# Reordering the state-space stage of a two-block transformer kernel: output projection rows between the mixing products, two exponent banks, an earlier rotary step

## The chip, the cores and the metric

The kernel runs on one core of a Trainium2 chip. The metric is the device time in microseconds (us) of one execution; smaller is better. The core has four compute engines with an instruction stream each: TensorE (PE in the profile, its weight loads PEld), VectorE (DVE), ScalarE (ACT) and GpSimd (POOL). A fifth stream, SyncE (SP), only issues transfers here. The engines meet through semaphores. TensorE writes its results into eight accumulation banks of 128 x 512 floats, `bank[0]` to `bank[7]`.

## The reference

512 tokens of width 1024 go through two blocks of two layers each, all in float32. The change touches the first block alone. One of its layers, cut to what matters:

```python
h = rms_norm(x, norm_mix_w[i])
q, k, v, z, xbc_raw, dt_raw = split(h @ w_in[i])          # 512, 128, 128, 512, 1024, 16 columns
q, k = axial_rope(rms_norm(q)), axial_rope(rms_norm(k))   # 8 query heads, 2 key heads of 64
attn_out = softmax(q @ k.T / 8) @ v                       # no mask
xbc = silu(depthwise_conv(xbc_raw, 5 taps) + bias)        # xs 512, B 2*128, C 2*128
dt = softplus(dt_raw + dt_bias)                           # two directions, 8 heads
# state-space scan in 4 chunks of 128 tokens, forward and backward:
#   inside a chunk   y += (C B^T * exp(decays)) @ (xs * dt)
#   between chunks   y += exp(..) * C @ state;   state = decay * state + B^T (xs * dt * ..)
y = (y_fwd + y_bwd + xs * d_skip) * silu(z)
y = y * rsqrt(mean(y * y, per group of 256) + EPS) * ssd_norm_w[i]
x = x + concat(attn_out, y) @ w_out[i]
x = x + (silu(g) * u) @ w_down[i]                         # g, u = rms_norm(x) @ w_gate, w_up; 2816 wide
```

The second block (windowed attention with a sink, differential attention, a convolution in the feed-forward) follows with other weights.

## The kernel before

**Products.** Every large product is three matmuls: activations and weights are split into a high and a low half, and `three` (L1658, L1659, L1660) adds high x high, low x high and high x low into one bank. The weights stream in by groups `g` of 1 MB into two alternating buffers. Of each group ScalarE makes the high half `w_hi` (`split_hi`, L341) and VectorE the low half `w_lo` (`split_lo`, L818), one group ahead of TensorE. TensorE enters a group through `enter(g)`, which waits for its halves.

**Order.** Each engine has one program that is written out by hand, with waits on semaphores between them. So an instruction runs when those in front of it on its engine are through and its semaphore has come, and moving a call in the source moves it in the stream. There is no scheduler.

**The first block's layer**, by groups from `g0`: queries (two groups), keys, values and step sizes, then the *channel stage*: groups `g0+4` to `g0+7` give the 1024 convolution channels as eight tiles `m` of 128 channels, and `g0+8`, `g0+9` the gate `z`. A half group fills one of banks 0 to 3. VectorE frees the bank of tile `m` in `conv_start(m)` (L1068), and adds the five taps with `conv_taps(m)` (L1077, one at each call's start on ScalarE, `conv_middle`, L560). ScalarE applies silu, and TensorE turns the tile to rows (`turn_channels(m)`). Among these calls VectorE also has the step sizes (`finish_dt`, L1089 to L1108: the softplus, with a logarithm that ScalarE computes at L586), the rotary steps `rope_a(t)` (L907 to L927, a 128-row tile `t` of queries and keys each), the low halves, and `state_coefs` (L1124). The last rows of queries that `rope_a(3)` makes are turned and rounded (L935) and then the first attention scores start (L1780).

**Attention** runs 20 half-steps `i`; TensorE is the busy engine there.

**The mixing stage** has eight passes `w = 2c + v`: chunk `c`, head group `v`. TensorE writes the exponents of unit `u` (16 units, two per pass, one per direction) into a bank of `E_BANKS` (L2029, L2030); ScalarE's `decay(u)` turns them to `a_e` (L642) and sets `dec_ready`; VectorE's `mixer(w)` adds the two directions (L1208) and multiplies by the scores `a_sm` (L1214), giving the mixing matrix `a_mx`; TensorE's `y_products(w)` (L2081, 4 matmuls of 64 columns) multiplies it into the bank `Y_BANKS[c % 2]`, on top of the skip term (L2073, from `skip_operand`, L1200). Beside this TensorE makes the chunks' states (`states(j, d)`, L2049), `scores(c)` (L2039) and the carried term `carried(c)` (L2064), which VectorE scales and adds (L1225 to L1232), then takes the products out (`take_y`, L1239) and gates them (`gate_y`, L1247). ScalarE squares the gated rows (`group_squares`, L662), VectorE makes the variance (`y_var`, L1253), GpSimd the factor (`group_factors`, L1548) and ScalarE applies it (`y_norm`, L670), which sets `yn_done`.

**Output projection.** `w_out` goes through four groups `g0+10` to `g0+13` (`IN_A = 10`). A half group is 8 row tiles `k`: 4 of the attention output `a_ot_hi`, `a_ot_lo`, ready early, and 4 of the normalised state-space output. `part(g, half, ks)` issues three matmuls per `k`. It runs the attention rows of the first two groups (2 groups x 2 halves x 4 x 3 = 48 matmuls), then waits for `yn_done`, turns the gated output on TensorE (L1763), and does the rest. The feed-forward follows.

## Time and profile before

| | us |
|---|---|
| runs | 2453.41, 2454.48, 2456.26 |
| median | 2454.48 |
| profiled execution | 2454.91 |
| its span in the trace | 2452.8 |

| engine | busy us | share |
|---|---|---|
| TensorE | 2397.9 | 98% |
| TensorE weight loads | 1977.3 | 81% |
| VectorE | 1437.0 | 59% |
| ScalarE | 933.7 | 38% |
| GpSimd | 249.6 | 10% |

The mean granted TensorE clock is 0.995 of full speed, and the transfers move 84 GB/s on average. How to read it: TensorE is busy nearly all the time, so its few pauses decide, not the other engines' shares. A row of a timeline gives the start of a group of like instructions in us, its length, engine, line, operation, operands (out<-in, partitions x elements) and their count; in square brackets stands the idle time in front of it and what ended that, by engine, tile and line. Matmuls are pipelined, so a row's length includes time in which the next is already under way. A releaser with a q (DVEq) is that engine's sequencer. The first block's second layer does the same work as its first, about 612 us later.

### The profile page before, as it was taken

The numbers are of one execution on the slowest core, as the hardware profiler recorded it, in microseconds if no ns is written. First come the engines' busy times: TensorE is split into PE (matmuls) and PEld (weight loads), VectorE is DVE, ScalarE is ACT, GpSimd is POOL, SyncE is SP. The second block draws the span as 40 slices with busy tenths as digits, with TensorE's granted clock in tenths as the row PEclk, the third lists the DMA queues.
The fourth block names the chain that finished last, engine by engine and source line by source line (L and its number), as shares of the span: only waits on it lengthen the run. The fifth ranks groups of instructions, "written<-read, shape, count | busy, mean of one in ns | idle before, by whom it ended". The sixth has DMA issues, their size and how long they took to land.

```text
span 2452.8 us, 30923 instructions
## 1 busy us (share of the span) xinstructions
PE 2397.9 (98%) x12492; PEld 1977.3 (81%) x12492; DVE 1437.0 (59%) x1976; ACT 933.7 (38%) x1468; POOL 249.6 (10%) x183
## 2 busy tenths in 40 slices
PE   8999999999999899999999999999999999999999
PEld 7777888888887688888887778888888777888887
DVE  6876543435587644343567766555466776655554
ACT  5564322223456432222344653222244475322222
POOL 3001100000200110000142411000012212000000
PEclk9999999999999999999999999999999999999999
DMA  5210222223211022222321102222232111222222
GB/s 186 69 36 18 103 86 103 88 101 105 102 69 36 18 103 96 93 103 87 111 95 69 36 28 93 103 88 101 99 107 89 67 36 43 95 101 89 103 89 101
DMA packets 31101, 205.32 MB, mean 84 GB/s; under 512 B 3440, under 2 KB 3568, under 8 KB 7408
## 3 DMA queue, kind: packets, MB, share of 16 engines
q1 hardware_dynamic: 30960, 203.35, 23.6%
q8 instruction: 99, 1.62, 0.3%
q14 instruction: 42, 0.34, 0.0%
HBM read 201.24 MB, written 2.10 MB: 83 GB/s over the span
## 4 chain that ended last, share of the span: by engine, by line
PE 87%; DVE 9%; DVEq 1%; issue 1%; ACT 1%; ACTq 0%; POOL 0%; DMA 0%; SPq 0%
PE bank L1658 26%; PE bank L1659 26%; PE bank L1660 26%; PE bank L1780 2%; PE bank L1841 2%; PE bank L1817 2%; DVE a_conv L1077 1%; DVE neg_max L1460 1%; PE bank L1763 1%; PE bank L1828 1%; DVE b_p L1472 1%; PE bank L2226 1%; DVE w_lo L818 1%; DVE h_mix_lo L935 1%; PE bank L2250 0%
## 5 line engine op out<-in xcount | busy, mean ns | idle before, releaser
L818 DVE TENSOR_TENSOR w_lo<-w_raw,w_hi 128x2048 fp32r<-128x2048 f32 (+1 forms) x180 | 411.1, 2284 | 392.8 <-ACT w_hi L341 392.1
L1658 PE MATMUL bank<-h_ffn_hi,w_hi 128*128 128x512 f32 x1408 | 549.2, 390 | 0.0
L1660 PE MATMUL bank<-h_ffn_hi,w_lo 128*128 128x512 f32 x1408 | 548.5, 390 | 0.0
L1659 PE MATMUL bank<-h_ffn_lo,w_hi 128*128 128x512 f32 x1408 | 548.4, 389 | 0.0
L341 ACT ACTIVATE w_hi<-w_raw 128x2048 fp32r<-128x2048 f32 (+1 forms) x180 | 340.9, 1894 | 451.9 <-PE bank L1660 424.0
L1660 PEld LDWEIGHTS bank<-h_ffn_hi,w_lo 128*128 128x128 f32 x1408 | 264.4, 188 | 55.1
L1658 PEld LDWEIGHTS bank<-h_ffn_hi,w_hi 128*128 128x128 f32 x1408 | 264.4, 188 | 54.5
L1659 PEld LDWEIGHTS bank<-h_ffn_lo,w_hi 128*128 128x128 f32 x1408 | 264.5, 188 | 54.3
L1659 PE MATMUL bank<-act_lo,w_hi 128*128 128x512 f32 x704 | 274.2, 389 | 0.0
L1658 PE MATMUL bank<-act_hi,w_hi 128*128 128x512 f32 x704 | 274.2, 389 | 0.0
L1660 PE MATMUL bank<-act_hi,w_lo 128*128 128x512 f32 x704 | 274.2, 389 | 0.0
L1535 POOL TENSOR_TENSOR sq_sum<-sq_sum,sq 128x512 f32<-128x512 f32 x56 | 95.3, 1701 | 1182.8 <-ACT sq L379 1181.5
L1658 PE MATMUL bank<-w_hi,h_mix_hi 128*128 128x512 f32 (+2 forms) x512 | 189.6, 370 | 9.1 <-DVE h_mix_lo L824 7.7
L482 ACT ACTIVATE act_hi<-up 128x512 fp32r<-128x512 f32 x88 | 55.7, 633 | 370.7 <-DVE up L997 370.7
L1660 PE MATMUL bank<-w_hi,h_mix_lo 128*128 128x512 f32 (+2 forms) x512 | 187.1, 365 | 0.0
L1659 PE MATMUL bank<-w_lo,h_mix_hi 128*128 128x512 f32 (+2 forms) x512 | 187.0, 365 | 0.0
L994 DVE TENSOR_TENSOR up<-bank,rstd_bc 128x512 f32<-128x512 f32 x88 | 60.8, 691 | 193.7 <-PE bank L1660 193.7
L1660 PEld LDWEIGHTS bank<-act_hi,w_lo 128*128 128x128 f32 x704 | 132.2, 188 | 27.5
L1659 PEld LDWEIGHTS bank<-act_lo,w_hi 128*128 128x128 f32 x704 | 132.2, 188 | 27.3
L1658 PEld LDWEIGHTS bank<-act_hi,w_hi 128*128 128x128 f32 x704 | 132.2, 188 | 27.3
L976 DVE TENSOR_TENSOR gate<-bank,rstd_bc 128x512 f32<-128x512 f32 x88 | 60.7, 690 | 118.1 <-PE bank L1660 116.3
L1658 PEld LDWEIGHTS bank<-w_hi,h_mix_hi 128*128 128x128 f32 x512 | 97.0, 189 | 25.1 <-DVE w_lo L1028 7.7
(330 smaller groups left out, 3406.1 us busy)
## 6 DMA issues: line engine op xcount, KB each, us to landing
w_raw<-weights SPq DMA_DIRECT2D x184, 1024.0 KB, 4.8
w_raw<-weights SPq DMA_DIRECT2D x4, 544.0 KB, 3.7
w_raw<-weights SPq DMA_DIRECT2D x8, 256.0 KB, 5.7
residual<-x_in SPq DMA_DIRECT2D x8, 256.0 KB, 5.6
x_out<-residual SPq DMA_DIRECT2D x8, 256.0 KB, 2.0
cst<-consts SPq DMA_DIRECT2D x1, 966.0 KB, 9.1
par_b<-params_b SPq DMA_DIRECT2D x1, 627.0 KB, 10.1
par_a<-params_a SPq DMA_DIRECT2D x1, 244.0 KB, 2.8
```

Source lines behind the costliest of these rows:

```text
L341: nc.scalar.activation(w_hi[s][:, cols], w_raw[s][:, cols], ACT.Copy).then_inc(w_hi_done, 1)
L482: act.activation(act_hi[:, 2 * i + j, :], up[j][:, :], ACT.Identity).then_inc(act_hi_done, 1)
L818: nc.vector.tensor_tensor(w_lo[s][:, cols], w_raw[s][:, cols], w_hi[s][:, cols].bitcast(F32), ALU.subtract).then_inc(w_ready, 1)
L976: nc.vector.tensor_tensor(gate[j][:, 1:SEQ + 1], bank[src][:, :], rstd_bc[:, :], ALU.mult).then_inc(bank_free[src], 1)
L994: nc.vector.tensor_tensor(up[j][:, :], bank[src][:, :], rstd_bc[:, :], ALU.mult).then_inc(bank_free[src], 1)
L1535: nc.gpsimd.tensor_tensor(sq_sum[:, :], sq_sum[:, :], sq[k % 2][:, :], ALU.add).then_inc(sum_done, 1)
L1658: mm(out, ahi, bhi, start=start, stop=False)
L1659: mm(out, ahi, blo, start=False, stop=False)
L1660: return mm(out, alo, bhi, start=False, stop=stop)
L1780: last = mm(bank[S_BANKS[i % 2][par_]][:, 0:nb * P], q_[rows, qs], k_[rows, ks], start=(n == 0), stop=(n == 2 and not masked))
L1817: last = nc.tensor.transpose(bank[PT_BANKS[par_]][:, b * P:(b + 1) * P], probs[u % 2][par_][:, b * P:(b + 1) * P], ident)
L1841: last = mm(bank[4][par_ * HD:(par_ + 1) * HD, j * P:(j + 1) * P], v_of(j // 2, k0 + b), pts[u % 2][par_][:, b * P:(b + 1) * P], start=(b ...
```

## The change

All calls keep their arithmetic but for `finish_dt`, which computes log(1 + p) with a shorter correction (five vector instructions and a wait in place of ten). The rest is order:

- ScalarE splits the high half of `g0+6` ahead of the logarithm, not behind the first channel tile; VectorE splits its low half right behind `finish_dt`.
- `state_coefs` moves from the channel stage to attention half-step 9; the skip operands of chunks 0 and 1 move from the mixing passes to half-step 18.
- `rope_a(3)` moves ahead of `conv_taps(4)`, from behind the low half of `g0+9`.
- TensorE turns channel tile 0 behind the first half of the third channel group, not behind the second.
- The exponents use two banks in place of three (`E_BANKS`) and are issued two per pass at its head; `Y_BANKS` becomes banks 7 and 4.
- 24 of the 48 matmuls of the output projection's attention rows (`out_rows`: first group, both halves) stand between the mixing products: three each in passes 2 to 5, six each in passes 6 and 7. `w_out` then starts with its second group.
- `y_var` of chunks 0 and 1 stands right behind `mixer(4)` and `mixer(6)`; ScalarE's squares of these chunks stand one decay later.

```diff
--- before.py
+++ after.py
@@ ScalarE
                 act.wait_ge(dt_v, 3 * lay + 1)
                 nc.scalar.activation(A["a_dt"][:, 1, :], A["a_dt"][:, 1, :], ACT.Exp, scale=-1.0)
                 nc.scalar.activation(tiny[:, 0:16], par[:, A_ALOG:A_ALOG + 16], ACT.Exp).then_inc(dt_s, 1)
+                split_hi(g0 + 6)
                 act.wait_ge(dt_v, 3 * lay + 2)
                 nc.scalar.activation(A["a_dt"][:, 3, :], A["a_dt"][:, 2, :], ACT.Ln).then_inc(dt_s, 1)
...
                 conv_middle(0)
-                split_hi(g0 + 6)
                 step_logs()
...
-                    nc.scalar.activation(A[f"a_e{w % 2}{d}"][:, :], bank[E_BANKS[u % 3]][:, :], ACT.Exp).then_inc(dec_ready, 1)
+                    nc.scalar.activation(A[f"a_e{w % 2}{d}"][:, :], bank[E_BANKS[u % 2]][:, :], ACT.Exp).then_inc(dec_ready, 1)
...
-                    if u in (8, 12):
+                    if u in (9, 13):
                         group_squares(u // 4 - 2)
@@ VectorE
                 def finish_dt():

-                    nc.vector.tensor_scalar(dt[4], dt[2], -1.0, None, ALU.add)
+                    nc.vector.scalar_tensor_tensor(dt[4], dt[2], -1.0, dt[1], ALU.add, ALU.subtract)
                     dve.drain()
-                    nc.vector.tensor_scalar(dt[5], dt[4], 0.0, None, ALU.is_equal)
-                    dve.drain()
-                    nc.vector.tensor_tensor(dt[4], dt[4], dt[5], ALU.add)
-                    dve.drain()
-                    nc.vector.reciprocal(dt[6], dt[4])
                     dve.wait_ge(dt_s, 2 * lay + 2)
-                    nc.vector.tensor_tensor(dt[3], dt[3], dt[5], ALU.add)
-                    dve.drain()
-                    nc.vector.tensor_tensor(dt[3], dt[3], dt[6], ALU.mult)
-                    dve.drain()
-                    nc.vector.tensor_tensor(dt[3], dt[3], dt[1], ALU.mult)
+                    nc.vector.tensor_tensor(dt[3], dt[3], dt[4], ALU.subtract)
                     dve.drain()
...
                 finish_dt()
+                split_lo(g0 + 6)
                 rope_a(2)
                 conv_start(1)
-                split_lo(g0 + 6)
                 conv_taps(0)
                 conv_start(2)
                 conv_taps(1)
                 remainder_rows()
-                state_coefs()
                 split_lo(g0 + 7)
...
                 conv_start(5)
+                rope_a(3)
                 conv_taps(4)
                 conv_start(6)
                 conv_taps(5)
                 conv_start(7)
                 split_lo(g0 + 9)
-                rope_a(3)
                 conv_taps(6)
                 conv_taps(7)
...
+                    if i == 9:
+                        state_coefs()
+                    if i == 18:
+                        skip_operand(0)
+                        skip_operand(1)
...
-                skip_operand(0)
                 for w in range(8):
                     c, v = divmod(w, 2)
                     mixer(w)
+                    if w in (4, 6):
+                        y_var(c - 2)
                     if w == 0:
...
-                        skip_operand(1)
...
-                    if w in (4, 6):
-                        y_var(c - 2)
@@ TensorE
-                for g in (g0, g0 + 1):
+                for g in (g0 + 1,) if rows_begun else (g0, g0 + 1):
                     enter(g)
...
-                        if g == 2 and half == 1:
-                            turn_channels(0)
-                            turn_channels(1)
+                        if g == 2:
+                            turn_channels(half)
...
-                    j = E_BANKS[u % 3]
-                    if u >= 3:
-                        pe.wait_ge(dec_ready, 16 * lay + u - 2)
+                    j = E_BANKS[u % 2]
+                    if u >= 2:
+                        pe.wait_ge(dec_ready, 16 * lay + u - 1)
...
+                def out_rows(half, k):
+
+                    ws = slice(k * COLS + half * P, k * COLS + half * P + P)
+                    three(bank[half][:, :], w_hi[0][:, ws], w_lo[0][:, ws], A["a_ot_hi"][:, k, :], A["a_ot_lo"][:, k, :], k == 0, False)
+
...
-                exponents(2)
                 pe.wait_ge(r_taken, 4 * lay + 4)
...
                     if w < 7:
+                        exponents(2 * w + 2)
                         exponents(2 * w + 3)
-                    if w < 6:
-                        exponents(2 * w + 4)
...
+                    if w == 2:
+                        enter(g0 + IN_A)
+                        pe.wait_ge(o_ready, 4 * lay + 4)
+                    if 2 <= w < 6:
+                        out_rows(0, w - 2)
+                    if w >= 6:
+                        pe.wait_ge(sm_ready, 4 * lay + 4)
+                        out_rows(1, 2 * w - 12)
+                        out_rows(1, 2 * w - 11)
                     y_products(w)
...
-E_BANKS = (5, 6, 7)
+E_BANKS = (5, 6)
 ST_BANKS = (3, 2)
-Y_BANKS = (0, 4)
+Y_BANKS = (7, 4)
```

TensorE, mixing stage of a layer, from the products of pass 6 to the end of mixing, before (`a_mx` mixing matrices, `a_state` the states for the carried term, `a_ot_hi` attention output, the first rows of `w_out`):

```order
L2081 MATMUL bank<-a_x,a_mx 128x64 x4
L2064 MATMUL bank<-a_state,a_bct 128x256 x2
L2081 MATMUL bank<-a_x,a_mx 128x64 x4
L1658 MATMUL bank<-a_ot_hi,w_hi 128x512
L1659 MATMUL bank<-a_ot_lo,w_hi 128x512
L1660 MATMUL bank<-a_ot_hi,w_lo 128x512
```

The same place now (old L2081 is L2073, L2064 is L2056, L1658 to L1660 are L1651 to L1653):

```order
L2073 MATMUL bank<-a_x,a_mx 128x64 x4
L2056 MATMUL bank<-a_state,a_bct 128x256 x2
L1651 MATMUL bank<-a_ot_hi,w_hi 128x512
L1652 MATMUL bank<-a_ot_lo,w_hi 128x512
L1653 MATMUL bank<-a_ot_hi,w_lo 128x512
L1651 MATMUL bank<-a_ot_hi,w_hi 128x512
L1652 MATMUL bank<-a_ot_lo,w_hi 128x512
L1653 MATMUL bank<-a_ot_hi,w_lo 128x512
L2073 MATMUL bank<-a_x,a_mx 128x64 x4
```

Before, only the carried matmuls stood between the products of passes 6 and 7, and the projection began behind them; now six matmuls of the projection's first rows stand ahead of the last products (and six ahead of those of pass 6).

VectorE, channel stage, before, from the bank read of tile 5 (`a_pad`) on:

```order
L1068 TENSOR_TENSOR a_pad1<-bank,rstd_bc 128x512
L1077 SCALAR_TENSOR_TENSOR a_conv0<-a_pad0,par_a,a_conv0 128x512 x4
L1068 TENSOR_TENSOR a_pad0<-bank,rstd_bc 128x512
L1077 SCALAR_TENSOR_TENSOR a_conv1<-a_pad1,par_a,a_conv1 128x512 x4
L1068 TENSOR_TENSOR a_pad1<-bank,rstd_bc 128x512
L818 TENSOR_TENSOR w_lo1<-w_raw1,w_hi1 128x2048
L907 TENSOR_TENSOR a_m1<-a_q,a_table 128x512
L907 TENSOR_TENSOR a_m1<-a_k,a_table 128x128
L916 TENSOR_TENSOR a_sqs<-a_q,a_table 128x8x16 x4
L916 TENSOR_TENSOR a_sqs<-a_k,a_table 128x2x16 x4
L920 TENSOR_TENSOR a_m1<-a_m1,a_sqs 128x640
L927 TENSOR_TENSOR a_q<-a_m1,head_rs 128x512
```

The same place now:

```order
L1068 TENSOR_TENSOR a_pad1<-bank,rstd_bc 128x512
L907 TENSOR_TENSOR a_m1<-a_q,a_table 128x512
L907 TENSOR_TENSOR a_m1<-a_k,a_table 128x128
L916 TENSOR_TENSOR a_sqs<-a_q,a_table 128x8x16 x4
L916 TENSOR_TENSOR a_sqs<-a_k,a_table 128x2x16 x4
L920 TENSOR_TENSOR a_m1<-a_m1,a_sqs 128x640
L927 TENSOR_TENSOR a_q<-a_m1,head_rs 128x512
L927 TENSOR_TENSOR a_kdup<-a_m1,head_rs 128x128
L927 TENSOR_TENSOR a_kdup<-a_m1,head_rs 128x64
L1077 SCALAR_TENSOR_TENSOR a_conv0<-a_pad0,par_a,a_conv0 128x512 x4
L1068 TENSOR_TENSOR a_pad0<-bank,rstd_bc 128x512
L1077 SCALAR_TENSOR_TENSOR a_conv1<-a_pad1,par_a,a_conv1 128x512 x4
```

The rotary step (`a_m1`, `a_q`, `a_kdup`) stood behind the bank reads of tiles 6 and 7 and the low half; now it is ahead of all three.

VectorE, mixing passes 4 and 5, before:

```order
L1208 TENSOR_TENSOR a_e00<-a_e00,a_e01 128x512
L1214 TENSOR_TENSOR a_mx0<-a_e00,a_sm 128x512
L1225 TENSOR_TENSOR a_y1<-bank,a_pfx 128x512
L1227 TENSOR_TENSOR sq1<-bank,a_pfx 128x512
L1232 TENSOR_TENSOR a_y1<-a_y1,sq1 128x512
L1239 TENSOR_TENSOR a_y1<-a_y1,bank 128x512
L1253 TENSOR_SCALAR tiny<-tiny 128x2
L1208 TENSOR_TENSOR a_e10<-a_e10,a_e11 128x512
```

The same now (old L1253 is L1243):

```order
L1198 TENSOR_TENSOR a_e00<-a_e00,a_e01 128x512
L1204 TENSOR_TENSOR a_mx0<-a_e00,a_sm 128x512
L1243 TENSOR_SCALAR tiny<-tiny 128x2
L1215 TENSOR_TENSOR a_y1<-bank,a_pfx 128x512
L1217 TENSOR_TENSOR sq1<-bank,a_pfx 128x512
L1222 TENSOR_TENSOR a_y1<-a_y1,sq1 128x512
L1229 TENSOR_TENSOR a_y1<-a_y1,bank 128x512
L1198 TENSOR_TENSOR a_e10<-a_e10,a_e11 128x512
```

The variance of chunk 0 moves from behind the carried and summed output (`a_y1`) to right behind the mixing matrix.

ScalarE, mixing stage, as a difference (`a_e` decays, `a_sm` scores, `sq` squares, `a_silu_z` the normalised output):

```order
 L642 ACTIVATE a_e<-bank 128x512 x3
 L650 ACTIVATE a_sm<-bank 128x256
+L642 ACTIVATE a_e<-bank 128x512
 L662 ACTIVATE sq,tiny<-a_y 128x256 x2
-L642 ACTIVATE a_e<-bank 128x512 x3
+L642 ACTIVATE a_e<-bank 128x512 x2
 L670 ACTIVATE a_silu_z<-a_y,tiny 128x256 x2
```

The squares of chunk 0 now come one decay later, and one decay fewer stands between them and the normalisation.

## Rows read from the trace of the kernel before

**Rows 1.** The page's first part: each engine's busy time, share of the span, instructions.

```profile
PE 2397.9 (98%) x12492; PEld 1977.3 (81%) x12492; DVE 1437.0 (59%) x1976; ACT 933.7 (38%) x1468; POOL 249.6 (10%) x183
```

**Rows 2.** TensorE's waits, 789 to 827 us: line <- releaser: us, times, longest.

```profile
PE bank L2081 <- DVE a_mx L1214: 4.9, 5, 2.1
...
PE bank L2064 <- DVEq L1194: 0.9, 1, 0.9
...
PE bank L2029 <- ACT a_e L642: 0.3, 1, 0.3
```

**Rows 3.** Timeline of TensorE, layer 1: start, us, line, operands, [idle before <-releaser].

```profile
821.23 1.11 PE L2081 MATMUL bank<-a_x,a_mx 128*128 128x64 f32 x8 [1.89 <-DVE a_mx L1214]
...
825.66 1.11 PE L2081 MATMUL bank<-a_x,a_mx 128*128 128x64 f32 x8 [2.10 <-DVE a_mx L1214]
...
826.58 0.48 PE L1658 MATMUL bank<-a_ot_hi,w_hi 128*128 128x512 f32 x1
...
836.50 1.03 PE L1763 MATMUL bank<-cst,a_silu_z 128*128 128x128 f32 x8
```

**Rows 4.** Stretches: us, busy PE, PEld, DVE, ACT, POOL, clock, DMA share, GB/s.

```profile
817.00:827.20 10.20, 5.80 (x32) 4.10 (x32) 7.21 (x12) 5.02 (x16) 1.07 (x1) 1.00 0.01 2
...
209.40:219.70 10.30, 9.14 (x28) 7.22 (x27) 6.25 (x12) 4.54 (x14) 2.46 (x3) 0.50 0.00 0
...
827.20:830.70 3.50, 3.50 (x10) 2.75 (x9) 1.62 (x4) 1.90 (x7) 0.86 (x2) 0.51 0.01 5
```

**Rows 5.** Timeline of TensorE, layer 0, end of mixing and first turn.

```profile
213.19 1.97 PE L2081 MATMUL bank<-a_x,a_mx 128*128 128x64 f32 x8 [1.16 <-DVE a_mx L1214]
...
225.44 1.04 PE L1763 MATMUL bank<-cst,a_silu_z 128*128 128x128 f32 x8
```

**Rows 6.** Timeline of ScalarE, layer 1, mixing stage.

```profile
816.14 0.91 ACT L670 ACTIVATE a_silu_z<-a_y,tiny 128x256 f32<-128x256 f32 x2 [4.77 <-POOL tiny L1548]
...
831.27 0.91 ACT L670 ACTIVATE a_silu_z<-a_y,tiny 128x256 f32<-128x256 f32 x2 [1.03 <-POOL tiny L1548]
```

**Rows 7.** Timeline of TensorE, layer 0, channel stage.

```profile
57.14 0.39 PE L1660 MATMUL bank<-h_mix_hi,w_lo 128*128 128x512 f32 x1
...
57.37 0.39 PE L1658 MATMUL bank<-h_mix_hi,w_hi 128*128 128x512 f32 x1
...
71.39 0.50 PE L1658 MATMUL bank<-h_mix_hi,w_hi 128*128 128x512 f32 x1 [0.52 <-DVE w_lo L818]
...
103.74 0.39 PE L1658 MATMUL bank<-w_hi,h_mix_hi 128*128 128x512 f32 x1
...
118.82 0.50 PE L1780 MATMUL bank<-h_mix_hi 64*128 64x512 f32 x2 [1.76 <-DVE h_mix_lo L935]
```

**Rows 8.** Timeline of VectorE, layer 0, channel stage.

```profile
60.11 0.20 DVE L1091 TENSOR_SCALAR a_dt<-a_dt 128x64 f32<-128x64 f32 x1
...
62.80 0.82 DVE L893 TENSOR_REDUCE ssq<-a_squares 128x10 f32<-128x640 f32 x1
...
79.65 0.29 DVE L1124 TENSOR_TENSOR a_coef<-a_dt,a_pfx 128x32 f32<-128x32 f32 x2
...
83.95 0.75 DVE L1077 SCALAR_TENSOR_TENSOR a_conv<-a_pad,par_a,a_conv 128x512 f32<-128x512 f32 x1 [0.86 <-ACT a_conv L560]
...
102.77 0.69 DVE L1068 TENSOR_TENSOR a_pad<-bank,rstd_bc 128x512 f32<-128x512 f32 x1
...
105.99 0.69 DVE L907 TENSOR_TENSOR a_m<-a_q,a_table 128x512 f32<-128x512 f32 x1
...
110.02 1.57 DVE L1077 SCALAR_TENSOR_TENSOR a_conv<-a_pad,par_a,a_conv 128x512 f32<-128x512 f32 x2
```

**Rows 9.** Timeline of ScalarE: layer 0's channel stage, then layer 1's mixing stage.

```profile
60.77 1.90 ACT L341 ACTIVATE w_hi<-w_raw 128x2048 fp32r<-128x2048 f32 x1
...
800.51 1.28 ACT L677 ACT_TABLE_LOAD   x1
...
801.80 1.06 ACT L677 ACTIVATE a_silu_z<-a_silu_z 128x1024 f32<-128x1024 f32 x1
```

More of the change, by code:

```diff
@@ L1846, in pair_attention, with w_out @@
                         behind[i]()
-            def w_out(lay, g0, base, n, ot_hi, ot_lo, src, mixed, count, high_banks):
+            def w_out(lay, g0, base, n, ot_hi, ot_lo, src, mixed, count, high_banks, rows_begun):
                 def part(g, half, ks):
@@ L2120, in _ @@
                         pe.wait_ge(o_free, 4 * lay + 4)
+                    if w == 2:
[7 more added lines that the diff above has]
+                        out_rows(1, 2 * w - 11)
                     y_products(w)
                 pe.wait_ge(dec_ready, 16 * lay + 16)
[L2123 removed]
+                w_out(lay, g0 + IN_A, base, 6, A["a_ot_hi"], A["a_ot_lo"], A["a_silu_z"], yn_done, 4 * lay + 4, (yi_free, 4 * lay + 4), True)
                 feed_forward(lay)
@@ L2252, in _ @@
                         last.then_inc(do_done, 1)
-                w_out(lay, g0 + IN_B, base, 14, B["b_ot_hi"], B["b_ot_lo"], B["b_dm"], mix_ready, l + 1, (do_free, 4 * l + 3))
+                w_out(lay, g0 + IN_B, base, 14, B["b_ot_hi"], B["b_ot_lo"], B["b_dm"], mix_ready, l + 1, (do_free, 4 * l + 3), False)
                 feed_forward(lay)
```

1 line of the change is left out of this document (removed).

## Prediction, written before the changed kernel was run

> **What bounds the kernel now.** First the table of engines: TensorE is busy 98% of the span [rows 1], and the chain of waits that ended last runs through it almost everywhere. So only two things can pay: stretches in which TensorE stands still, and stretches in which it runs at half clock. I went through its timeline for every row with an idle time in front, in the two layers of the first block, the only ones that the change touches. They sit in two places, the same in both layers.
>
> The larger is the mixing stage. Between 789 and 827 us the view of waits puts nearly all of TensorE's idle time down to VectorE's mixing tiles, five waits of 4.9 us together; with one wait of 0.9 and two of 0.3 us the stage has 8 gaps of 6.4 us [rows 2]. The timeline shows the longest: 2.10 us before the last mixing products, at 825.66 [rows 3]. A 512-column matmul's row is 0.39 us long while the next starts 0.23 us after it [rows 7], so each gap costs about 0.16 more than its idle row: 8 gaps, 7.7 us per layer.
>
> Then the clock. In layer 0 TensorE's granted clock is 0.50 (1.2 GHz) for 10.3 us, in layer 1 0.51 for 3.5 us [rows 4], and each stretch begins right behind the long waits at the end of mixing. What it costs is read from one piece of work in both layers, from the start of the last mixing products to the turn of the gated output: 225.44 - 213.19 = 12.25 us in layer 0 [rows 5], 836.50 - 825.66 = 10.84 us in layer 1 [rows 3]. The piece is 0.92 us of mixing products and 36 matmuls at 0.227, 8.16, and 0.1 for the switch: 9.2 at full clock. So the clock costs 3.1 and 1.7 us, together 4.7.
>
> The second place is the channel stage. TensorE waits 0.52 us for a low weight half at 71.39 and 1.76 us for VectorE's last turned query row before the first scores at 118.82 [rows 7]. VectorE is nearly without a pause there.
>
> **The change, part by part.** All times are of one layer; the sum doubles them.
>
> *Channel stage.* The shorter step-size arithmetic first. It now takes 2.69 us, 60.11 to 62.80 [rows 8]. Five of ten instructions stay, at the steps of those rows about 0.3 each for the first three and 0.1 for the last two. But the high half of group g0+6 now stands on ScalarE ahead of the logarithm that they need. It may start when TensorE ends group g0+4, whose last matmul is the one at 57.14 [rows 7], at about 57.6; it lasts 1.90 as at 60.77, a table load behind it 1.28 [rows 9] and a 64-element step some 0.2: 61.0. VectorE, ready at 60.4, waits 0.6 and ends at 61.9, 0.9 earlier than now. Next, the low half of g0+6 follows at once and ends near 64.1, long before TensorE asks for it at 70.9: its wait of 0.52 goes. The state coefficients leave the stage: from 79.65 to 80.02 with the drain in front, 0.45 [rows 8]; in the attention VectorE has room for them. VectorE's wait of 0.86 at 83.95 is for ScalarE behind the channel transposes; the first of these now follows half a group earlier on TensorE, so I let it vanish.
>
> Then the last rotary step, 105.99 to 110.02, 4.03 us [rows 8], is put in front of the fifth channel tile's taps. Queued behind it are taps 4 and 5, the reads of banks 2 and 3 by tiles 6 and 7, and the low half of g0+9. Bank 3 is the tight one. TensorE starts writing it at 103.74 [rows 7], and VectorE gives it free at 102.77 + 0.69 = 103.46 [rows 8]: 0.28 us of slack. With the change VectorE frees it at 103.46 + 4.03 - 0.9 - 0.45 - 0.86 = 105.3, TensorE is there at 103.2, and a new wait of about 2 us opens; I take 1.9. What it buys: VectorE comes to the turned rows 2.2 us earlier, TensorE to the first scores 1.4 later, so the wait of 1.76 closes. Net: -0.5 + 1.9 - 1.8 = -0.4. The ends: without the new wait -2.2; with it and the old wait still open +1.4. A table load rule of the Trainium skill bears on this place. The trace shows a load of 1.28 us at 800.51 and its function's start at 801.80, 1.29 later [rows 9]: the load is the whole price. The Trainium skill (ScalarE: Activation LUTs, section What ACT_TABLE_LOAD costs) adds a drain of about 1.38 us to each switch; by it the logarithm and everything behind it on VectorE would come 1.4 later, and the time is that of the rival below.
>
> *Mixing stage.* Per pass w of eight TensorE issues two exponents, then scores, carried terms and the like, then the mixing products. Three edits take work out of its waits. (a) The skip operands (0.6 us each) go from VectorE's mixing passes into its wait for the last attention block. (b) The group variance of chunks 0 and 1 is taken right behind mixer 4 and 6, no longer behind some 2.9 us of carried and summed output. Now ScalarE waits 4.77 us at 816.14 for GpSimd's factor [rows 6], the decays behind it come late, and TensorE stands 1.89 us before the products at 821.23 [rows 3]; the factor now comes earlier and the squares stand behind one more decay. (c) 24 matmuls of the output projection's first rows, 5.44 us, stand ahead of the products: three each in passes 2 to 5, six each in 6 and 7. In these passes TensorE had five gaps and, from here on, enough work of its own to cover them.
>
> What remains. Passes 0 to 2 get no filler, so the waits for the second and third states and for the first carried term stay, 0.3 to 0.9 in the trace. And one grows: the third exponents now come behind the first states and the skip term, ScalarE's decay 2 stands ahead of its copy of the first states, so the second states wait for the copy, about 1.0. I count 2.8 us of waits left ahead of the last products. They then end 2.8 + 5.44 - 7.7 = 0.5 us later than now.
>
> Behind them the cover is gone. Now 36 matmuls (8.3 us with the switch) hide the chain take, gate, squares, variance, factor, norm: from the end of the products at 826.58 [rows 3] to 831.27 + 0.91 = 832.2 [rows 6], 5.6 us, of which 0.45 is VectorE still busy with chunk 2's variance; I take 5.3. With 12 matmuls left (2.8 us) TensorE waits a new 2.5 us there, and the turn comes 5.3 instead of 8.3 behind the products. Net: +0.5 + 5.3 - 8.3 = -2.5. The ends: -5.0 if the left-over 2.8 us of waits were mostly gone, +2.4 if the fillers hid nothing.
>
> *Clock.* The long waits ahead of the last products go, but a wait of 2.5 takes their place. In layer 1 half clock followed the 2.10 us before 825.66; the 1.89 before 821.23 had left it at full [rows 3, 4], and so had the 1.76 at 118.82 in layer 0 [rows 7]. So I expect a fall again, with dense matmuls right behind it, which is layer 1's case now: 1.7 us, not layer 0's 3.1. Gain 4.7 - 3.3 = 1.4 over both.
>
> *Two exponent banks.* Exponents u waits for decay u-2 instead of u-3, but each pair is issued one slot later, so it waits for the same decays as now; the bank is worth nothing by itself and gives bank 7 to the products so that bank 0 is free for the projection. Later groups of the projection, the feed-forward and the second block keep their work; no DMA is added, and the weights' transfers are not near the path (DMA share 0.01 at the end of mixing [rows 4]).
>
> **Sum.** 2 x (-0.4 - 2.5) - 1.4 = -7.2. Against the profiled execution's 2454.9 us (span 2452.8) that is 2447.7; the median of the runs, 2454.48, lies 0.4 under it, so I give **2447.3**.
>
> **Rivals.** *The clock holds.* If one wait of 2.5 between dense stretches doesn't bring it down, 3.3 more comes back: 2444.0. For it: the 1.76 one was harmless; against: 2.5 is longer than the 2.10 that brought it down. *The fillers only partly hide.* If VectorE's mixing chain, not TensorE, sets the pace to the end, the products come 2.5 later than I say: 2447.3 + 5 = 2452.3. For it: VectorE is busy 7.21 of 10.2 us there [rows 4]. *The channel stage turns bad*: bank 3's wait comes and the first scores still wait: +1.8 per layer, 2451. For it: the slack of 0.28. *Slower: a serial round.* With two banks the exponents of pass w+1 are issued only at the head of pass w. If VectorE is through its other work before these exponents (0.46) and the second decay (0.5) are done, every pass gets longer by 0.96, seven times, 6.7 per layer: 2447.3 + 13.4 = 2460.7. It decides from the point where VectorE's carried work, 3.7 us per pass at most, is shorter than exponents, two decays and two handovers, some 1.8; the rows speak against it in all but the even passes. *The table load* with a drain: +1.4 per layer through bank 3, 2450.1. *The change doesn't do what it says*: the built order shows all the moves; if the gains are given back whole, 2454.5.
>
> **How the numbers follow.** Forecast 0.45, clock holds 0.22, partly hidden 0.13, channel stage 0.08, serial round 0.06, table load 0.03, nothing 0.03. The range takes in the forecast with its terms' play, the clock case and the channel case: 2443.5 to 2451.3, with the serial round, the empty case and most of the partly hidden one left out. A measurement here tells 0.2%, 4.9 us: faster means under 2449.6. Forecast and clock case give 0.67, and of the three cases between 2450 and 2452.3 about 0.09 falls under the line: faster 0.76, within 0.17, slower 0.07.
>
> **What would show it.** In the profile after: no wait for a low weight half before group g0+6; a TensorE wait of 1.6 to 2.1 us on VectorE's channel tile halfway through group g0+8 and none before the first scores; about 1 us before the second states; no wait before the mixing products from pass 2 on; 2.3 to 2.8 us before the first turn of the gated output, with a clock of 0.5 for some 3.5 us behind it; ScalarE's waits for GpSimd's factor near 4.8 gone for chunks 0 and 1. Wrong would be mixing waits left in passes 4 to 7 (then the fillers don't cover) or a first turn without a wait (then the chain is shorter than its rows).

## The result: 14.4 us less, twice the forecast

| | before | after |
|---|---|---|
| median of the runs, us | 2455.22 | 2440.79 (2439.73 to 2443.41) |
| profiled execution, us | 2454.91 | 2443.41 |
| its span, us | 2452.8 | 2441.6 |
| mean granted TensorE clock in it | 0.995 | 0.998 |

The ratio of the runs is 0.9944, 95% interval 0.993 to 0.9958. The forecast was 2447.3 in a range of 2443.5 to 2451.3: the sign was right, the time lies 2.7 us under the range. A second set of five runs of the changed kernel gave 2440.81.

The engines' busy times of the kernel after, to be read beside [rows 1]: TensorE's fell by 6.7 us with the same count of matmuls. By the sums below, 4.7 us of that can be time at the lower clock in the first block.

```profile
PE 2391.2 (98%) x12492; PEld 1971.7 (81%) x12492; DVE 1434.6 (59%) x1966; ACT 934.2 (38%) x1468; POOL 252.0 (10%) x183
```

TensorE's waits over the whole span of the kernel after, both layers together (line <- releaser: us, times, longest), the rows that belong to the first block. The old mixing waits [rows 2] are gone. New are the turn (L1756), the bank (a_pad), the copied first states (a_state) and a channel tile's silu (a_bct).

```profile
PE bank L1756 <- ACTq L672: 3.3, 2, 1.7
...
PE bank L1651 <- DVE a_pad L1068: 2.7, 2, 1.3
...
PE bank L2056 <- DVEq L1184: 1.9, 2, 1.0
PE bank L2041 <- ACT a_state L655: 1.6, 2, 0.8
...
PE bank L1952 <- ACT a_bct L569: 0.8, 2, 0.6
```

TensorE's timeline after, layer 0 in the channel stage and at the end of mixing, then layer 1 (last products and first turn), to be read beside [rows 3, 5, 7]:

```profile
100.91 0.66 PE L1952 MATMUL bank<-cst,a_bct 128*128 128x128 f32 x4 [0.25 <-ACT a_bct L569]
...
105.67 0.50 PE L1651 MATMUL bank<-w_hi,h_mix_hi 128*128 128x512 f32 x1 [1.34 <-DVE a_pad L1068]
...
119.04 0.50 PE L1773 MATMUL bank<-h_mix_hi 64*128 64x512 f32 x2
...
213.17 1.00 PE L2073 MATMUL bank<-a_x,a_mx 128*128 128x64 f32 x8
...
218.64 1.09 PE L1756 MATMUL bank<-cst,a_silu_z 128*128 128x128 f32 x8 [1.66 <-ACTq L672]
...
819.15 1.00 PE L2073 MATMUL bank<-a_x,a_mx 128*128 128x64 f32 x8
...
824.62 1.09 PE L1756 MATMUL bank<-cst,a_silu_z 128*128 128x128 f32 x8 [1.67 <-ACTq L672]
```

From the last products to the first turn it is now 5.47 us in both layers, where it was 12.25 and 10.84. Two windows of the kernel after over the stretches that held half clock before (columns as in [rows 4], the clock is the last but two): no half clock is left in the first block.

```profile
209.40:219.70 10.30, 8.64 (x51) 7.31 (x50) 4.16 (x8) 4.01 (x14) 1.40 (x2) 1.00 0.01 2
816.80:827.00 10.20, 8.53 (x47) 7.06 (x47) 3.84 (x8) 4.91 (x14) 1.40 (x2) 1.00 0.00 1
```

**Where the time went**, by differences between starts of TensorE rows in the profiled executions, layer 0 / layer 1. "Channel" runs from the small matmuls that turn the norm's factor (36.51 in layer 0 of before) to the first scores, "mixing" from there to the last mixing products (attention included), "tail" from those to the first turn of the gated output. The table also holds the experiments that follow. They ran on three chips, on which the kernel before had medians of 2455.2, 2455.4 and 2454.8 us.

| kernel | channel | mixing | tail | median us |
|---|---|---|---|---|
| before | 82.3 / 82.0 | 94.4 / 94.4 | 12.25 / 10.84 | 2455.2 |
| after | 82.2 / 82.5 | 94.1 / 94.0 | 5.47 / 5.47 | 2440.8 |
| turn_only | 81.6 / 81.3 | 94.4 / 94.4 | 10.80 / 9.20 | 2452.7 |
| dt_only | 81.2 / 81.2 | 94.6 / 94.4 | 10.94 / 11.23 | 2452.5 |
| var_only | 82.3 / 82.0 | 91.0 / 91.1 | 10.82 / 12.43 | 2448.3 |
| rows_back | 82.2 / 82.5 | 91.3 / 91.2 | 9.21 / 12.38 | 2447.8 |
| var_back | 82.3 / 82.6 | 94.7 / 94.6 | 6.59 / 6.59 | 2447.4 |
| long_wait | 82.2 / 82.6 | 94.2 / 94.0 | 5.66 / 5.66 | 2453.5 |
| turn_late | 81.2 / 81.5 | 94.1 / 94.0 | 5.47 / 5.46 | 2443.1 |
| rope_back | 80.1 / 80.4 | 94.1 / 94.0 | 5.47 / 5.46 | 2438.2 |
| rows_late | 82.2 / 82.5 | 92.8 / 92.6 | 5.47 / 5.47 | 2439.9 |
| rope_rows | 80.1 / 80.4 | 92.8 / 92.7 | 5.47 / 5.47 | 2435.1 |
| copy_first | 80.1 / 80.4 | 91.6 / 92.1 | 5.47 / 4.97 | 2435.0 |

At full clock the tail with 36 matmuls is 9.2: rows_back shows it in layer 0, turn_only in layer 1. So of the tail's change, 3.7 us per layer come from work and 3.1 and 1.6 from the clock. The first block's sum is 2 x (-0.3 - 3.7) + 0.5 - 4.7 = -12.2 us. The two profiled executions differ by 11.5 us, the medians by 14.4; where the last 2 us between the medians lie, no run shows. The second block, which the change doesn't touch, varies by itself: from its first score matmul to the end of the span it takes 1132.4 us in the profile of before and 1133.0 and 1131.3 in the two profiles of the changed kernel.

### The profile page after: what moved, and what is told of

Read it like the earlier page. It is cut to its first block, busy times and chain, and to the rows that moved or that the text cites. A ratio compares the mean times of both kernels' runs of the same rounds, so it can differ in the third digit from the quotient of the medians.

```text
span 2441.6 us, 30909 instructions
## 1 busy us (share of the span) xinstructions
PE 2391.2 (98%) x12492; PEld 1971.7 (81%) x12492; DVE 1434.6 (59%) x1966; ACT 934.2 (38%) x1468; POOL 252.0 (10%) x183
## 4 chain that ended last, share of the span: by engine, by line
PE 89%; DVE 7%; issue 1%; ACT 1%; DVEq 1%; POOL 0%; ACTq 0%; DMA 0%; SPq 0%
PE bank L1651 26%; PE bank L1653 26%; PE bank L1652 26%; PE bank L1773 2%; PE bank L1834 2%; PE bank L1810 2%; DVE a_conv L1077 1%; PE bank L1756 1%; DVE neg_max L1453 1%; PE bank L1821 1%; DVE b_p L1465 1%; PE bank L2230 1%; PE bank L2254 0%; PE bank L2056 0%; PE bank L2073 0%
## 5 line engine op out<-in xcount | busy, mean ns | idle before, releaser
L1651 PE MATMUL bank<-h_ffn_hi,w_hi 128*128 128x512 f32 x1408 | 548.6, 390 | 0.0
L1653 PE MATMUL bank<-h_ffn_hi,w_lo 128*128 128x512 f32 x1408 | 547.8, 389 | 0.0
L1653 PEld LDWEIGHTS bank<-h_ffn_hi,w_lo 128*128 128x128 f32 x1408 | 264.3, 188 | 55.1
L1651 PEld LDWEIGHTS bank<-h_ffn_hi,w_hi 128*128 128x128 f32 x1408 | 264.3, 188 | 54.4
L1651 PE MATMUL bank<-act_hi,w_hi 128*128 128x512 f32 x704 | 273.9, 389 | 0.0
L1653 PE MATMUL bank<-act_hi,w_lo 128*128 128x512 f32 x704 | 273.9, 389 | 0.0
L1651 PE MATMUL bank<-w_hi,h_mix_hi 128*128 128x512 f32 (+2 forms) x512 | 189.9, 371 | 11.7 <-DVE h_mix_lo L824 7.6
L1653 PE MATMUL bank<-w_hi,h_mix_lo 128*128 128x512 f32 (+2 forms) x512 | 187.1, 365 | 0.0
L1651 PEld LDWEIGHTS bank<-act_hi,w_hi 128*128 128x128 f32 x704 | 132.1, 188 | 27.4
L1653 PEld LDWEIGHTS bank<-act_hi,w_lo 128*128 128x128 f32 x704 | 132.1, 188 | 27.3
L1651 PEld LDWEIGHTS bank<-w_hi,h_mix_hi 128*128 128x128 f32 x512 | 97.0, 189 | 28.5 <-DVE w_lo L1028 7.6
```

The source lines that it names most:

```text
L1651: mm(out, ahi, bhi, start=start, stop=False)
L1653: return mm(out, alo, bhi, start=False, stop=stop)
```

## The experiments

All kernels but the single edits of before (var_only, turn_only, dt_only) start from the changed kernel. The changed kernel again:

> The changed kernel once more, as the measure for the other runs of this study, about 2440.8 us against 2455.2 of before. Its profiled run of the first time had a granted clock of 0.998 and two stretches at half clock, both in the second block; its other runs had 0.999 to 1.0. If those stretches come and go from one execution to the next, this profile shows another set of them, and in the first block none, with 1.7 us of wait before the first turn of the gated output.

2440.81 us (2440.26 to 2442.09), ratio 0.9944. The first block's rows repeat within 0.1 us, and no half clock is in it. In the second block half clock began at nearly the same two places as in the first profile (1384.3 and 1988.5, now 1380.9 and 1988.5), but for other lengths: 3.4 and 6.8 us the first time, 6.8 and 3.4 now.

**1. The matmuls put back (rows_back).**

```diff
                     if w == 0:
                         pe.wait_ge(o_free, 4 * lay + 4)
-                    if w == 2:
-                        enter(g0 + IN_A)
-                        pe.wait_ge(o_ready, 4 * lay + 4)
-                    if 2 <= w < 6:
-                        out_rows(0, w - 2)
-                    if w >= 6:
-                        pe.wait_ge(sm_ready, 4 * lay + 4)
-                        out_rows(1, 2 * w - 12)
-                        out_rows(1, 2 * w - 11)
                     y_products(w)
```

and `w_out` starts with its first group again.

> The changed kernel with the 24 matmuls of the output projection back behind the mixing stage; variance, squares, skip operands, exponents and banks as changed. Theory 1 (the matmuls are the cover, as forecast): the five gaps of the mixing stage come back, 4 us or more per layer, while the 2.5 us before the first turn go; and the clock falls again; 2446 to 2450. Rival (ScalarE's earlier normalisation took the gaps away, the matmuls lie where no gap is left): only about 0.3 us before the products of pass 2 and 1.6 us before those of pass 7 are left, against the 1.7 us before the first turn that goes, so the time at full clock is that of the changed kernel within 1.5 us, 2440 to 2442; if half clock comes back it adds 1.7 to 3.1 per layer, up to 2446. The trace tells which part is which.

2447.76 us (2446.35 to 2448.7), ratio 0.997 [0.9959, 0.9981]. TensorE's timeline of rows_back in layer 0 and a window of layer 1:

```profile
205.77 1.00 PE L2073 MATMUL bank<-a_x,a_mx 128*128 128x64 f32 x8
...
209.76 1.10 PE L2073 MATMUL bank<-a_x,a_mx 128*128 128x64 f32 x8 [2.03 <-DVE a_mx L1204]
...
218.97 1.04 PE L1756 MATMUL bank<-cst,a_silu_z 128*128 128x128 f32 x8
```

```profile
816.80:823.80 7.00, 7.00 (x22) 5.86 (x23) 2.69 (x6) 3.63 (x12) 1.39 (x2) 0.53 0.00 1
```

Theory 1 falls for the gaps: without the matmuls, the products of pass 6 (205.77) stand without a wait; of the long ones only the 2.03 before pass 7 is left. At full clock the way from the first scores to the turn is 100.5 us against 99.6 with the matmuls: they are worth 0.9 us per layer of work. Of the other 5 us between the medians, 3.2 are the half clock that came in layer 1 right behind the 2.03 us wait and lasted 6.8 us (tail 12.38 against 9.2); in layer 0 the same wait brought none. Some 2 us more lie in the second block: it takes 1133.5 us here with 17 us of half clock, and 1131.3 in after_again with 11.

**2. The variance put back (var_back).**

```diff
                     mixer(w)
-                    if w in (4, 6):
-                        y_var(c - 2)
...
                         gate_y(c - 1)
+                    if w in (4, 6):
+                        y_var(c - 2)
...
-                    if u in (9, 13):
+                    if u in (8, 12):
                         group_squares(u // 4 - 2)
```

> The changed kernel with the variance of chunks 0 and 1 back behind the carried and summed output and the squares one decay earlier, as before; the 24 matmuls stay between the products. Theory 1 (the matmuls are the cover): the gaps stay covered, at most the last link grows; 2440.8 to 2442. Rival (the earlier variance is the cure): ScalarE waits some 4 us for the factor again, the products of passes 5 and 7 come late behind it, and the wait before the first turn grows from 1.7 to some 2.6; about 1.2 us per layer slower, 2443.3, more if the clock falls as well.

2447.39 us (2446.09 to 2450.24), ratio 0.9973 [0.9961, 0.9984]. ScalarE's normalisation in layer 0, in var_back and then in the kernel after:

```profile
204.66 0.91 ACT L670 ACTIVATE a_silu_z<-a_y,tiny 128x256 f32<-128x256 f32 x2 [3.52 <-POOL tiny L1541]
```

```profile
200.59 0.91 ACT L670 ACTIVATE a_silu_z<-a_y,tiny 128x256 f32<-128x256 f32 x2
...
208.50 0.91 ACT L670 ACTIVATE a_silu_z<-a_y,tiny 128x256 f32<-128x256 f32 x2
```

With the old place ScalarE waits 3.5 us for GpSimd's factor, as it did 4.77 in [rows 6]; with the new one it doesn't wait. The rival holds: 1.7 us per layer at full clock (scores to turn 101.3 against 99.6), 0.5 before the last products and 1.1 in the tail, since chunk 2's squares queue behind the late normalisation. The medians differ by 6.6 us: these rows give 3.3 of it and half clock behind the turn in layer 0 another 1.6. The turn's row of var_back:

```profile
220.78 1.49 PE L1756 MATMUL bank<-cst,a_silu_z 128*128 128x128 f32 x8 [2.17 <-ACTq L672]
```

Behind this wait came half clock in layer 0 (0.50 from 221.3 to 224.7) and none in layer 1, with the same wait of 2.17 us.

**3. The variance alone, in the kernel before (var_only).** The reverse of the diff above, on the kernel before.

> The kernel before with one edit alone: the variance of chunks 0 and 1 right behind mixer 4 and 6, the squares one decay later. Nothing else of the change. Theory (the earlier factor frees ScalarE's decays, and this is what took the gaps out of passes 5 and 6): of the long waits only the last stays, 2.0 us before the products of pass 7; from the first scores to the first turn some 3.4 us per layer less at full clock, 103.5 in place of 106.6 and 105.2 less what the clock does. About 2448.5 us against 2455.2, 2445 if half clock also goes. Rival (the 24 matmuls and the moved skip operands do it): under 1 us per layer, 2453.5 or more.

2448.3 us (2445.43 to 2450.22), ratio 0.997 [0.9958, 0.9982]. TensorE's waits on the mixing tiles in layer 0 of var_only; in layer 1 of before it was 4.9 in five [rows 2]:

```profile
PE bank L2081 <- DVE a_mx L1214: 2.7, 3, 2.0
```

The last products come 3.3 us earlier per layer. One edit of two places gives 3.3 of the 4.1 us at full clock that the whole mixing part gave; all the rest of that part without it, the matmuls among it (var_back), gives 103.6 - 101.3 = 2.3. The two fill the same gaps, so together they make 4.1, not 5.6. The moved skip operands and the two exponent banks were not run by themselves, but rows_back has them and var_only does not, and its way to the last products is 0.3 and 0.2 us longer: together they bring nothing there. What they cost is in part the wait for the copied first states (0.81), see copy_first.

**4. The rotary step put back (rope_back).**

```diff
                 conv_start(5)
-                rope_a(3)
                 conv_taps(4)
...
                 split_lo(g0 + 9)
+                rope_a(3)
                 conv_taps(6)
```

> The changed kernel with the last rotary step put back behind the low half of g0+9; all else as changed. Theory 1 (the early rotary step is a loss): VectorE has the same work ahead of the last turned rows either way, so the step buys nothing there and only holds bank 3 back; the 1.34 us wait in g0+8 goes, the first scores still come without a wait of over 0.3, since the shorter step-size arithmetic and the moved coefficients already give VectorE its 1.4 us of slack. About 1.5 us per layer better, 2437.8 against the changed kernel's 2440.8. Rival (the forecast's view, the early step closes the wait of 1.76 before the first scores): the bank wait goes but 1.4 to 1.8 us before the first scores return; within 0.6 us of 2440.8.

2438.18 us (2435.72 to 2439.8), ratio 0.9931 [0.9918, 0.9943]. Between 50 and 120 us TensorE has no wait left; the first scores of rope_back, to be read beside 119.04 after and 118.82 [rows 7]:

```profile
116.44 0.50 PE L1773 MATMUL bank<-h_mix_hi 64*128 64x512 f32 x2
```

The channel stage is 2.1 us shorter in both layers: the early rotary step was a loss. It held bank 3 back (1.34 us), and the taps and silu of tile 4, which stand right behind it, as well (0.25 and 0.57). The medians differ by 2.6 us, not 4.2, and their intervals overlap; the rows carry this one.

**5. What paid in the channel stage: turn_only, dt_only, turn_late.**

```diff
-                        if g == 2 and half == 1:
-                            turn_channels(0)
-                            turn_channels(1)
+                        if g == 2:
+                            turn_channels(half)
```

> The kernel before with one edit alone: TensorE turns channel tile 0 behind the first half of the third channel group and tile 1 behind the second. Theory (VectorE's waits of 0.86 at 83.95 and 0.62 at 99.45 for ScalarE, which is late with the taps behind both transposes, are what holds the last turned rows back): the wait of 1.76 before the first scores closes to under 0.5, the channel stage goes from 82.3 and 82.0 to 80.9 and 80.7 us; about 1.3 us per layer. Rival (VectorE's own work is what sets the end of this stage, so only the shorter arithmetic and the moved coefficients help): under 0.4 us per layer.

2452.67 us (2449.49 to 2453.41), ratio 0.9988 [0.9979, 0.9997]. The stage got 0.7 us per layer shorter, and the wait before the first scores fell to 1.1 (0.7 in layer 1): in between the two theories' numbers.

> The kernel before with the shorter step-size arithmetic alone. VectorE gets 1.2 us of work less, ahead of the third rotary step. Theory (a wait for ScalarE later in the stage takes it back): the wait for the low half of g0+6, 0.52, closes, the one before the first scores stays; 0.3 to 0.6 us per layer. Rival (VectorE sets the end of the stage): 1.2 to 1.7 us per layer, the channel stage at 81 us or less.

2452.46 us (2449.22 to 2454.57), ratio 0.9987 [0.9978, 0.9996]; 1.15 and 0.8 us per layer, again in between. Of VectorE's 1.2 us of saved work 0.7 came back as a longer wait for ScalarE, which was 0.86 at 83.95 [rows 8]. VectorE in layer 0 of dt_only:

```profile
82.76 1.58 DVE L1077 SCALAR_TENSOR_TENSOR a_conv<-a_pad,par_a,a_conv 128x512 f32<-128x512 f32 x2 [1.57 <-ACT a_conv L560]
```

> The kernel of the run with the rotary step at its old place, and TensorE's turn of tiles 0 and 1 both behind the second half of the third channel group again. It leaves the shorter step-size arithmetic, the moved coefficients and the earlier halves of g0+6. Theory (the turn carries most of the stage's gain): 1.3 us or more before the first scores are back, the channel stage at 81.5 us or more in place of 80.1 and 80.4. Rival (VectorE's shorter work carries it): 80.5 or less.

2443.1 us (2439.34 to 2443.78), ratio 0.9949 [0.9937, 0.9962]; the stage is 1.1 us per layer longer than in rope_back, and 1.4 and 1.8 us stand before the first scores. Neither theory holds whole. The turn is worth 0.7 alone and 1.1 behind the shorter arithmetic: each removes a wait that hid part of the other's gain.

**6. The twelve matmuls of passes 6 and 7 spread otherwise (rows_late).**

```diff
-                    if w >= 6:
+                    if w == 7:
                         pe.wait_ge(sm_ready, 4 * lay + 4)
-                        out_rows(1, 2 * w - 12)
-                        out_rows(1, 2 * w - 11)
+                        out_rows(1, 0)
+                        out_rows(1, 1)
                     y_products(w)
+                out_rows(1, 2)
+                out_rows(1, 3)
```

> The changed kernel with the twelve matmuls of the second half group spread otherwise: none in pass 6, six between the last carried matmuls and the products of pass 7, six behind those products. Theory (the matmuls of passes 6 and 7 hold back products that VectorE has ready, and the chain to the first turn starts behind them): the last products come 1.1 to 1.5 us earlier, the chain of 4.66 behind them stays, the wait before the first turn falls from 1.7 to some 0.6; 1.1 to 2.0 us per layer, 2437 to 2438.6 against 2440.8. Rival (VectorE is the later one in pass 7): the products gain nothing and a wait opens ahead of them; 2440.8.

2439.89 us (2437.16 to 2442.26), ratio 0.9935 [0.9923, 0.9948]. The last products and the first turn of rows_late, layer 0:

```profile
212.34 1.00 PE L2073 MATMUL bank<-a_x,a_mx 128*128 128x64 f32 x8
...
217.81 1.09 PE L1756 MATMUL bank<-cst,a_silu_z 128*128 128x128 f32 x8 [0.29 <-ACTq L672]
```

The last products come 1.4 us earlier, the chain behind them is still 5.47, and its wait is 0.29. The median moved by 0.9 only and the intervals overlap; the rows show 2.8 for both layers.

**7. One longer wait, for the clock (long_wait).** The last twelve matmuls ahead of the first turn stand behind it.

> The changed kernel with the last twelve matmuls ahead of the first turn put behind it, so that one wait of 1.7 + 2.8 = 4.4 us stands in otherwise dense work. At full clock that costs 2.8 us per layer, 2446.4. Theory 1 (the clock follows the length of one wait, as forecast): half clock behind it in both layers, 3.4 us or more each, cost 1.7 each, 2449.8. Rival (the clock follows how thin the work of a longer stretch is; one wait does nothing): no half clock in the first block, 2446.4.

2453.48 us (2448.54 to 2455.41), ratio 0.9987 [0.9978, 0.9995]. Its wait in layer 0, then two windows inside the wait (layers 0 and 1) and two behind it:

```profile
PE bank L1756 <- ACTq L672: 4.7, 1, 4.7
```

```profile
218.30:219.50 1.20, 0.00 (x0) 0.02 (x1) 0.00 (x0) 0.91 (x2) 0.00 (x1) 0.50 0.00 0
829.30:831.00 1.70, 0.00 (x0) 0.00 (x0) 0.00 (x0) 0.91 (x2) 0.57 (x1) 0.50 0.00 0
...
218.60:225.50 6.90, 5.99 (x19) 5.10 (x20) 1.50 (x2) 2.02 (x4) 0.00 (x0) 0.53 0.01 2
829.00:836.00 7.00, 4.92 (x16) 4.28 (x17) 1.60 (x3) 2.28 (x4) 0.70 (x1) 0.52 0.00 0
```

The rival falls, since it said that one wait does nothing: here one wait in dense work brings half clock in both layers, 6.8 us of it. Theory 1 foresaw that, but at 1.7 us lost each. The clock fell while TensorE still waited (at 218.3 and 829.3, the waits end at 219.51 and 831.08), so 1.2 and 1.8 us of the half clock cost nothing. By rows each layer is 5.5 and 5.2 us longer than in after_again: 2.8 for the twelve matmuls, 2.7 and 2.4 for the clock, 10.8 us for both layers. The medians differ by 12.7; the rest is not in the first block.

That the length of one wait decides is not shown by this. The second block, which no run edits, has one wait of 2.2 us per layer, and half clock began with its end or at most 2.1 us behind it in 23 of the 28 layers of all traces. But seven times it began elsewhere, with no single wait of over 1.45 us (three times) or over 0.95 us (four times) in the 4 us ahead. TensorE in rows_back, layer 1 of the second block, and a window of the clock behind these rows:

```profile
1941.11 0.66 PE L1756 MATMUL bank<-cst,b_qb 128*128 128x128 f32 x4 [0.48 <-ACT b_vb L500]
1942.34 0.39 PE L1773 MATMUL bank<-b_kd_hi,h_mix_hi 64*128 64x256 f32 x2 [0.57 <-ACT b_p L448]
```

```profile
1943.00:1949.80 6.80, 6.31 (x39) 4.90 (x38) 3.37 (x8) 4.42 (x15) 0.00 (x0) 0.50 0.01 2
```

**8. The best of both, and the copy (rope_rows, copy_first).** rope_rows has the diffs of 4 and 6.

> Both: the last rotary step at its old place and the twelve matmuls spread as in the run above. The places are far apart, so the gains should add: 2.1 us per layer from the rotary step (the channel stage to 80.1 and 80.4 us) and 1.1 to 2.0 from the matmuls; 2434 to 2436 us, if the second block's half clock is as in the other runs. If the two share a bound it is 2437 or more.

2435.11 us (2434.05 to 2436.27), ratio 0.9915 [0.9902, 0.9929], which lies clear of the changed kernel's interval. The gains add by rows: 80.1 and 80.4, 92.8 and 92.7.

copy_first adds to it:

```diff
                 for u in range(2, 16):
+                    if u == 2:
+                        first_state(0)
+                        first_state(1)
                     decay(u)
...
-                    if u == 2:
-                        first_state(0)
-                        first_state(1)
```

> The best kernel so far (the last rotary step at its old place, the twelve matmuls spread around pass 7) with one edit more: ScalarE copies the first states ahead of decay 2, not behind it. The forecast says that the second states wait about 1.0 us (measured 0.8) for this copy since decay 2 stands ahead of it. If so the wait goes, and since VectorE waits for the same copy (2.67 us at 182.17) the whole mixing stage comes 0.9 to 1.1 us earlier per layer: 2433 us against 2435.1. If VectorE's later work or decay 2 binds instead, under 0.3 per layer.

2435.03 us (2431.08 to 2435.84), ratio 0.9916 [0.9902, 0.9929]. The second states stand without a wait, and from the scores to the turn it is 97.1 and 97.0 us against 98.2 and 98.1, as expected. The median doesn't show it; that it is hidden by the clock is likely, not shown. This profiled execution had three stretches of half clock, 17 us together, behind the first turn of layer 1. The stretch from that turn to the end of the span is 1618.9 us here and 1613.0 in rows_late, with the same instructions:

```profile
814.70:2433.60 1618.90, 1593.01 (x8092) 1318.37 (x8092) 928.35 (x1213) 577.13 (x881) 173.41 (x114) 0.99 0.24 85
```

```profile
822.40:2435.40 1613.00, 1585.77 (x8092) 1312.88 (x8092) 926.75 (x1213) 577.25 (x881) 173.30 (x114) 1.00 0.24 85
```

## Why the prediction was wrong in size, step by step

The forecast's -7.2 us are -0.8 in the channel stage, -5.0 from the first scores to the turn at full clock, and -1.4 of clock. The first block's rows give +0.5, -8.0 and -4.7. So the forecast missed by +1.3, -3.0 and -3.3, and the loss in the channel stage hid part of the miss; the last 2.2 us to the medians are the open ones. The step that failed first is the length of the chain behind the last products, 5.3 us in the forecast and 4.7 measured: it mis-sized the tail and the wait before the turn, and by the wait the clock.

- **Clock: -1.4 forecast, -4.7 in the first block.** The step that failed is "a wait of 2.5 takes their place ... so I expect a fall again". The wait was mis-sized: it measured 1.66 and 1.67. Over all traces, in the first block's two layers: no half clock behind the mixing stage in the 14 layers where the longest wait was 1.67 or less; half clock in 11 of the 14 where it was 1.9 or more (4.7: two of two). In six of these 14 two waits of 1.2 to 2.1 us follow each other, so the length of one wait is not all that differs. This was the rival "the clock holds" (2444.0), reached by another reason than it gave. The bound that I drew between 1.89 and 2.10 came from layer 1 alone and is wrong: in layer 0 of before half clock began at 209.4, behind this row and ahead of the last products at 213.19.

```profile
208.75 1.37 PE L2081 MATMUL bank<-a_x,a_mx 128*128 128x64 f32 x8 [1.90 <-DVE a_mx L1214]
```

The 3.8 us of half clock ahead of 213.19 cost nothing, since TensorE waits for VectorE there in any case (94.4 us to the last products in both layers). So the price of 3.1 stands.

- **Tail: 8.3 to 5.3 behind the end of the products forecast, 8.3 to 4.7 measured** (5.47 less 0.8 from the products' start to their end). I took the chain from layer 1 of before, where it was 5.6, and took off 0.3. But in before, chunk 1's normalisation stood ahead of chunk 2's squares on ScalarE and waited 4.77 us for its factor; the earlier variance took that out as well. The cause was named in the same paragraph and not carried through to the chain. var_back shows it: with the old place the tail is 1.1 longer, 6.59. ScalarE in layer 1 of before:

```profile
825.37 0.91 ACT L670 ACTIVATE a_silu_z<-a_y,tiny 128x256 f32<-128x256 f32 x2 [4.77 <-POOL tiny L1548]
826.38 0.42 ACT L662 ACTIVATE sq<-a_y 128x256 f32<-128x256 f32 x1
```

- **Mixing up to the last products: +0.5 forecast, -0.3 measured.** The left-over waits are 0.81, 0.31 and 0.95, 2.1 in place of 2.8.
- **Who does it.** I gave the gaps to the matmuls. By var_only the earlier variance alone takes 3.3 us per layer, and by rows_back the matmuls add 0.9 of work. What they also do is turn the last wait of 2.03 us into one of 1.66, behind which no half clock came. The sum did not price these edits apart, so the wrong cause changed no term of it: that is luck.
- **Channel stage: -0.4 forecast, -0.1 and +0.6 measured.** Right: no wait for the low half, a bank wait (1.34 for 1.9), the first scores without a wait. VectorE freed bank 3 1.8 us later in the stage than before, as forecast; TensorE was there later than forecast, so the wait is shorter. Not seen: tile 4's silu comes late too (0.25, 0.57). Mis-valued: the move was costed as one sum with the savings. Apart, the savings are 2.2 and 1.6, and the early rotary step spends 2.1 of them: layer 0's 2.2 is the forecast's own lower end, "without the new wait -2.2" (its terms, 0.5 and 1.8, make 2.3).
- **Table load.** VectorE in layer 0 of the kernel after waits 0.75 us for the logarithm, where 0.6 was forecast and 2.0 would follow with a drain on top of the load (on ScalarE the load starts at 59.87 and the logarithm at 61.16, 1.29 later):

```profile
61.45 0.23 DVE L1094 TENSOR_TENSOR a_dt<-a_dt 128x64 f32<-128x64 f32 x1 [0.75 <-ACT a_dt L582]
```

By the Trainium skill (ScalarE: Activation LUTs, section What ACT_TABLE_LOAD costs) a drain of about 1.38 us would come on top of the load; this row leaves no room for it.

- **Serial round and the fillers that only partly hide:** neither came. From pass 3 to the first turn TensorE doesn't wait at all.
- **The base.** I made the sum against one execution with a clock of 0.995. The kernel before ran 12, 16 and 21 times on three chips, at 2451.9 to 2457.3, 2452.7 to 2458.0 and 2452.9 to 2457.6 us; the shortest runs have a mean clock of 0.997, the longest 0.993. On the first chip they fall in two groups (five up to 2452.6, seven from 2455.1), on the others they don't. So this kernel's time has some 5 us of play that goes with the clock, and the range had no room for that.

Left open: why the same wait of 1.9 to 2.2 us brings half clock in one layer and not in the other, what brings it where no wait is long, and what sets its length (3.4, 6.8 or 10.2 us here). Where the last 2 us of the gain lie is not shown either.

## What to carry to other kernels

When a wait sits behind a chain over three engines, look for the engine that is blocked in order by the chain's slowest link: here two moved calls, one on VectorE and one on ScalarE, gave more by rows than all else in the stage without them, 24 moved matmuls included. Cost an early move apart from the savings that travel with it; the moved step may spend them. In the first block a wait of 1.9 us or more on TensorE cost its length and, in 11 of 14 layers, 1.6 to 3.2 us of half clock, so cutting a wait from 2.1 to 1.7 was worth more there than cutting one from 1.7 to 0.3. Do not carry 1.9 over as a bound: the second block had half clock without such a wait.

## What was unexpected in the hardware

A single wait of 4.7 us in dense work brought 6.8 us of half clock in both layers, which began before the wait was over. And the clock in unchanged code varied from run to run: from the first turn of layer 1 to the end, the same 8092 matmuls took 1613.0 us without half clock and 1618.9 with 17 us of it. It did not fall just anywhere: in all 14 traces every stretch of half clock in the second block, but for the last microsecond of the span, began within 3 us of one of four places in the program, two per layer; each execution had some of them, and rows_late had none.
